# A state-space layer scanned token by token, and by chunks of four tokens

## The reference, cut to what matters

```python
lam_bar = jnp.exp(lam * dt)
b_bar = ((lam_bar - 1.0) / lam)[..., None] * b
bu = jnp.einsum('bsgh,gph->bsgp', uf, b_bar)
# states[t] = lam_bar * states[t-1] + bu[t], over 512 tokens
y = jnp.einsum('bsgp,ghp->bsgh', states, c).real + d_skip * uf
y = gelu(y)
```

## Time and profile before

| | |
|---|---|
| median of 3 runs | 3060.92 us (3058.44 to 3063.92) |
| the profiled execution | 3063.83 us |
| its span, first to last instruction | 3062.0 us |
| mean granted TensorE clock | 0.962 |
| TensorE busy | 2899.5 us (95%) |
| VectorE busy | 1527.1 us (50%) |
| ScalarE busy | 967.5 us (32%) |
| GpSimd busy | 175.9 us (6%) |
| state-space stage, 1966.57 to 2250.60 us | 284.03 us |
| in it: TensorE, VectorE, GpSimd busy | 238.09, 262.39, 131.75 us |
| in it: mean granted clock | 0.81 |

### The profile page before, as it was taken

One profiled execution on the slowest core, in us unless ns is written; L12 is line 12 of the kernel. 1 busy time (PEld: TensorE's weight loads), 2 busy tenths in 40 slices (PEclk: granted clock), 3 DMA queues, 4 the chain that ended last, 5 costly groups with the idle time before them and its releaser, 6 DMA issues.

```text
span 3062.0 us, 42173 instructions
## 1 busy us (share of the span) xinstructions
PE 2899.5 (95%) x17870; PEld 2326.6 (76%) x17870; DVE 1527.1 (50%) x2550; ACT 967.5 (32%) x1556; POOL 175.9 (6%) x136
## 2 busy tenths in 40 slices
PE   7999999999999999999999999788996899999999
PEld 5875678888888877767788888645574688888887
DVE  3464444433233344347565355599967633443333
ACT  2144543221122232146443233311125422332222
POOL 2000000100000000000000000154400000000000
PEclk9999999999999999999999999877877999999999
DMA  6232010222333211110112333011120032322322
GB/s 251 88 106 67 28 35 29 96 104 105 116 107 118 86 63 56 62 35 1 55 56 90 103 110 110 29 42 41 50 79 28 28 97 96 103 70 86 107 91 88
DMA packets 67787, 238.46 MB, mean 78 GB/s; under 512 B 7440, under 2 KB 10640, under 8 KB 66960
## 3 DMA queue, kind: packets, MB, share of 16 engines
q1 hardware_dynamic: 67312, 234.20, 22.5%
q10 hardware_dynamic: 288, 1.57, 0.2%
HBM read 233.64 MB, written 2.10 MB: 77 GB/s over the span
## 4 chain that ended last, share of the span: by engine, by line
PE 85%; DVE 10%; ACT 3%; issue 2%; DMA 1%; POOL 0%; SPq 0%; DVEq 0%; ACTq 0%; POOLq 0%
PE PSA L646 82%; PE PSA L952 1%; DVE WS L2071 1%; PE PSA L1213 1%; DVE Y L2693 1%; DMA Y<-in_early 1%; DVE Y L2690 1%; DVE stat L2774 1%; DVE Y L2689 1%; ACT Y L1939 0%; PE PSA L1447 0%; DVE HS L2241 0%; ACT WS L1532 0%; ACT Y L1946 0%; DVE Y L2703 0%
## 5 line engine op out<-in xcount | busy, mean ns | idle before, releaser
L646 PE MATMUL PSA<-HS,WS 128*128 128x512 f32 (+1 forms) x6672 | 1367.6, 366 | 19.2 <-DVE HS L2241 12.7
L646 PEld LDWEIGHTS PSA<-HS,WS 128*128 128x128 f32 x6672 | 1139.4, 191 | 250.8 <-issue 45.5
L2071 DVE TENSOR_TENSOR WS<-W,WS 128x1024 fp32r<-128x1024 f32 (+2 forms) x318 | 363.2, 1144 | 583.6 <-ACT WS L1532 582.4
L1532 ACT ACTIVATE WS<-W 128x1024 fp32r<-128x1024 f32 (+2 forms) x318 | 313.9, 989 | 846.9 <-PE PSA L646 487.6
L646 PE MATMUL PSA<-YS,WS 128*128 128x512 f32 (+1 forms) x2232 | 471.1, 372 | 3.5 <-DVE YS L2806 3.5
L646 PEld LDWEIGHTS PSA<-YS,WS 128*128 128x128 f32 x2232 | 393.1, 189 | 79.4 <-DVE YS L2806 3.9
L646 PE MATMUL PSA<-Y 128*64 128x128 f32 (+8 forms) x2048 | 319.7, 374 | 56.1 <-DVE Y L2703 36.5
L646 PEld LDWEIGHTS PSA<-Y 128*64 128x64 f32 (+3 forms) x2048 | 176.8, 164 | 153.1 <-issue 83.7
L1516 ACT ACTIVATE Y<-PSA 128x512 f32<-128x512 f32 (+3 forms) x73 | 50.2, 692 | 329.2 <-PE PSA L646 325.8
L646 PE MATMUL PSA<-HS,YS 128*128 128x512 f32 (+1 forms) x696 | 130.7, 346 | 4.5 <-issue 4.1
L646 PEld LDWEIGHTS PSA<-HS,YS 128*128 128x128 f32 x696 | 109.7, 194 | 22.7 <-issue 7.7
(11 more groups left out here) (298 smaller groups left out, 2586.6 us busy)
## 6 DMA issues: line engine op xcount, KB each, us to landing
W<-in_weights SPq DMA_DIRECT2D x396, 512.0 KB, 3.5
Y<-in_early SPq DMA_DIRECT2D x4, 2048.0 KB, 19.5
W<-in_weights SPq DMA_DIRECT2D x24, 256.0 KB, 2.7
X<-in_x SPq DMA_DIRECT2D x4, 768.0 KB, 20.4
W<-in_weights SPq DMA_DIRECT2D x24, 128.0 KB, 2.3
Y<-in_ssm ACTq DMA_DIRECT2D x1, 1024.0 KB, 7.2
out<-X SPq DMA_DIRECT2D x1, 1024.0 KB, 5.8
C<-in_consts SPq DMA_DIRECT2D x1, 948.5 KB, 33.0
```

The lines of the kernel that those rows point to most:

```text
L646: return pe.matmul(out, lhsT, rhs, start=first, stop=last)
L1532: act.activation(split_home(n)[:, 0, 0:f], W[:, c % W_RING, 0:f], ACT.Copy)\
L2071: tt(home[:, 1, 0:f], W[:, c % W_RING, 0:f], home[:, 0, 0:f].bitcast(F32), ALU.subtract)\
```

## The change

The 512 tokens are cut into 128 chunks of four. What four tokens bring into the state at a chunk's end is a sum over the four steps j, with the input matrix multiplied by the transition to the power 3 - j. TensorE makes that sum in PSUM (`chunk_inputs`), so that one state tile has 128 columns in place of 512, and the four state tiles of 128 channels are worked on together: `chunk_states(q)` on VectorE replaces four steps of before, with 8 scans of 128 columns. The output has two parts. From the state before the chunk comes the product with the output matrix times the transition to the power j + 1 (`OB`, made by GpSimd in `observe`). From the tokens inside the chunk comes a sum of lag matrices, one of 128 x 128 for each of the lags 0 to 3, which TensorE makes once (`lag_kernels`), ScalarE copies block by block (`keep_kernels`), and into whose lag 0 VectorE adds the skip as a diagonal (`add_skip`). `read_out(q)` adds both in one PSUM bank for four state tiles, and ScalarE takes it out with the gelu.

The input matrices of the four steps are made in feed-forward 1 on VectorE (`next_inputs`) and turned by TensorE there (`turn_inputs`, 32 transposes in place of 8), behind gate and up tiles 14, 15 and 17. The projection's tiles "q2" move behind "kc" and "vc". GpSimd makes 4 sets of phasors in place of 16, and 4 sets of output matrices. Tables move to other buffers.

```diff
-            state_inputs(0)
-            for i in range(SSM_T):
-                if i + 1 < SSM_T:
-                    state_inputs(i + 1)
-                for key in keys_at_state_tile(i):
-                    tile(key, ("in2",) + key, HS2, LAT)
-                read_out(i)
+            def chunk_inputs(q):
...
+                u = by_step(U[:, q, :])
                 for ri in range(2):
+                    for j in range(STEP):
+                        for r in range(4):
+                            key, rows = keys[r // 2], slice(32 * r, 32 * r + 32)
+                            at = S * (r % 2) + CHUNKS * ri
+                            ins = mm(PS[slot(key)][:, at:at + CHUNKS], BBT[rows, j, ri, q, :], u[rows, :, j],
+                                     j == 0, j == STEP - 1)
...
+            def lag_kernels():
...
+                for later in range(2):
+                    if later:
+                        pe.wait_ge(observed, value("observed", 2))
+                    for q in range(4):
+                        for ri in range(2):
+                            for r in range(4):
...
+                                if later:
+                                    ins = mm(half[:, 2 + q // 2::2, :], BB[:, ri, i, :], OB[:, 0:STEP - 1, ri, i, :],
+                                             ri == 0, ri == 1)
+                                else:
+                                    ins = mm(half[:, q // 2, :], BB[:, ri, i, :], SSMW[:, 2 + ri, i, :],
+                                             ri == 0, ri == 1)
...
+            def read_out(q):
...
+                ps, u = by_step(PS[slot(key)][:, 0:S]), by_step(U[:, q, :])
+                for l in range(STEP):
+                    mm(ps[:, :, l:STEP], lag_kernel(l, q), u[:, :, 0:STEP - l], l == 0, False)
+                pe.wait_ge(observed, value("observed", 3))
+                pe.wait_ge(states_ready, value("states_ready", q))
+                for j in range(STEP):
+                    for ri in range(2):
+                        for r in range(4):
+                            ins = mm(ps[32 * r:32 * r + 32, 1:CHUNKS, j], OB[:, j, ri, 4 * q + r, :],
+                                     XB[q % 2][:, ri, r * CHUNKS:(r + 1) * CHUNKS - 1],
+                                     False, j == STEP - 1 and ri == 1)
...
+            chunk_inputs(0)
+            for n, key in enumerate(IN2[4:28]):
+                tile(key, ("in2",) + key, HS2, LAT)
+                if n % 4 == 2 and n < 12:
+                    chunk_inputs(n // 4 + 1)
+                if n == 4:
+                    lag_kernels()
+                if n % 4 == 1 and 5 <= n <= 17:
+                    read_out(n // 4 - 1)
...
+                if n % 4 == 1 and 5 <= n <= 17:
+                    q = n // 4 - 1
+                    copy_out(("y", q), U[:, q, :], n=S, func=ACT.Gelu_apprx_tanh)
...
+            pool.wait_ge(b_bar, value("b_bar", 0))
+            pool.wait_ge(psum_filled[slot(last)], turn(last))
+            chunk_phasors(0)
+            pool.wait_ge(psum_filled[slot(("u", 3))], turn(("u", 3)))
+            chunk_phasors(1)
+            for j in range(STEP):
+                observe(j)
+            for q in (2, 3):
+                pool.wait_ge(states_ready, value("states_ready", q - 2))
+                chunk_phasors(q)
...
+            def chunk_states(q):
...
+                for h in range(2):
...
+                    tt(vr_, g[:, 0], er_, ALU.mult)
+                    tt(zi_, g[:, 0], ei_, ALU.mult)
+                    tt(zr_, g[:, 1], ei_, ALU.mult)
+                    tt(vi_, g[:, 1], er_, ALU.mult).then_inc(psum_drained[slot(key)], 1)
...
+                for t in range(4):
...
+                    dve.tensor_tensor_scan(zr[:, cols], decay, vr[:, cols], 0.0, ALU.mult, ALU.add)
+                    ins = dve.tensor_tensor_scan(zi[:, cols], decay, vi[:, cols], 0.0, ALU.mult, ALU.add)
...
+            for n, key in enumerate(IN2[4:28]):
+                if n % 4 == 0 and n < 16:
+                    chunk_states(n // 4)
+                in2(key)
+                if n == 4:
+                    add_skip()
```

More of the change, by code:

```diff
@@ L234, in build @@
         b_bar = sem("b_bar")
+        observed = sem("observed")
+        kernels_ready = sem("kernels_ready")
         branches_split = sem("branches_split")
@@ L1300, in _ @@
-            for ri in range(2):
-                pe.wait_ge(psum_drained[slot(("b_turned", ri))], turn(("b_turned", ri)))
-            def state_inputs(i):
-                q, rows = i // 4, slice(32 * (i % 4), 32 * (i % 4) + 32)
-                take(("bu", i))
-                if turn(("bu", i)) > 1:
-                    pe.wait_ge(psum_drained[slot(("bu", i))], turn(("bu", i)) - 1)
-                ps = PS[slot(("bu", i))]
-                for ri in range(2):
-                    ins = mm(ps[:, ri * S:(ri + 1) * S], BBT[rows, ri, q, :], U[rows, q, :], True, True)
-                ins.then_inc(psum_filled[slot(("bu", i))], 1)
@@ L1313, in read_out @@
-            def read_out(i):
-                pe.wait_ge(states_ready, value("states_ready", i))
-                rows = slice(32 * (i % 4), 32 * (i % 4) + 32)
-                take(("y", i))
-                if turn(("y", i)) > 1:
-                    pe.wait_ge(psum_drained[slot(("y", i))], turn(("y", i)) - 1)
-                ps = PS[slot(("y", i))]
-                for ri in range(2):
-                    ins = mm(ps[rows, 0:S], SSMW[:, 2 + ri, i, :], SB_[:, 8 + ri, :], ri == 0, ri == 1)
-                ins.then_inc(psum_filled[slot(("y", i))], 1)
@@ L1917, in _ @@
             more_weights(("cmp1", 1, 3))
-            for q in range(4):
-                act.wait_ge(psum_drained[slot(("y", 4 * q + 3))], turn(("y", 4 * q + 3)))
-                act.activation(U[:, q, :], U[:, q, :], ACT.Gelu_apprx_tanh).then_inc(ssm_out, one("ssm_out", q))
             act.wait_ge(psum_filled[slot(("kcmp",))], turn(("kcmp",)))
@@ L2698, in _ @@
+                link(ins)
+                read = ("cb", 0) if q < 2 else ("y", q - 2)
+                dve.wait_ge(psum_filled[slot(read)], turn(read))
                 tt(xr, zr, er, ALU.mult)
```

275 lines of the change are left out of this document (170 added, 105 removed).

## The result

The changed kernel takes 2974.44 us, median of 4 runs (2973.28 to 2976.32), against 3061.73 us for the kernel before on the same chip. The ratio is 0.9716, 95% interval 0.97 to 0.9733. The forecast was 2977 us. The profiled executions differ by as much: spans of 3062.0 and 2974.5 us.

What follows compares the result with a forecast made beforehand. VectorE was taken to bound the state-space stage before, TensorE after. New stage 181.3 + 10.1 + 5 = 196.4 us for 284.0, saving 87.6; feed-forward 1 adds 4.1; 2980.3 profiled, 2977 us as median, range 2955 to 3020.

Steps and rivals of the forecast that it cites:

- the sum by stretches: State-space stage 87.6 us shorter, 4.1 us added in feed-forward 1 for 32 transposes, nothing taken behind the stage.
- VectorE set the pace of the stage before: In the state-space stage before, VectorE was busy 262.39 of 284.03 us and TensorE waited 36.5 us for it.
- TensorE's work: In the new stage at full clock: projection tiles, chunk inputs, both read-out products and lag matrices, 181.3 us together.
- Both rivals on this block: On `chunk_inputs`: strided records take twice their time (16%, 3020 us); four row groups overlap, 7 us not 28 (9%, 2956).
- Strided operands: Rival, 16%: strided reads in chunk inputs and gapped PSUM writes in read-outs double such records' time, adding 43 us: 3020.
- Waits: TensorE's idle time left in the new stage, at its start, first read-out, ring slots and end: 10.1 us together.
- VectorE's set of 14.0 us: VectorE's work for four state tiles in the new stage: products, sums at 1.45 us, scans at 0.45 us, 14.0 us.
- The late-helper rival: Rival, 11%: GpSimd's sets take 15 us, TensorE waits 17 (2994); or 128-column scans cost as much as 512-column ones (3013).
- Clock: In the new stage, three of TensorE's waits may each cost 1.7 us of lowered clock: 5 us.
- the signs that the prediction named for being wrong: Idle TensorE ahead of `observed` or `weights_split`, half clock behind the small blocks, a VectorE set of over 16 us.
- Gain not there: Rival, 1%: VectorE remains the bound, which would need sets of some 60 us; about 3061 us.
- the half clock rival: Rival, 4%: small products put the stage at 1.2 GHz, 181 us of work become 362; the kernel ends at 3153.

Runs made afterwards that it cites:

- group_by_group: The changed kernel with the chunk sums' loops turned round, all four steps of one 32-row group before the next: 2998.27 us, ratio 0.9795 to the kernel before.

## Why the prediction was right, point by point

- **The time** of 2977 was 2.6 us off, and the sum by stretches came out close as well: stage -90.3 against -87.6, the start of the stage +4.9 against +4.1, behind it -2.1 against 0. That the last two agree says little, as they are within what one execution differs from the next. What was forecast right is the mechanism, VectorE's work off the path and TensorE the bound; that the number came within 3 us is luck, as the points below show.
- **VectorE set the pace of the stage before**: shown. Without its scans the kernel is 41 us faster, without most of GpSimd's work beside it 43, and the first of these edits takes only 5 from the changed kernel.
- **TensorE's work**, 181.3 us, was 15 too much. The tiles, 129.6, measured 5.47 us each, 131.3. The lag products, 9.1, measured 10.0; the state products, 9.6, measured 7.5; the lag matrices, 4.8, measured 2.0. The term that was mis-sized is `chunk_inputs`: 28.2 us (110 ns a record), measured 15.3 (60 ns). The nearest row had two row groups in turn, and I took its price for four. Both rivals on this block were true at once: four groups run together (31 ns a record with whole runs, 8.0 us in all, where that rival had 7), and the strided operand doubles it. Each multiplied the wrong base, so that neither gave the time.
- **Strided operands** cost 4 x 1.82 us on the chunk inputs and 4 x 0.25 on the lag products, 8 us, not 43. The Trainium skill's rule on lines of 16 bytes in SBUF ("SBUF — State Buffer", section "Door 1: The DMA port swizzle") agrees with 60 against 31 ns. Its sentence there that any gap in PSUM slows matmuls significantly does not agree with the trace: 1.94 us with and without.
- **Waits**, 10.1 us, measured 21.6: 11.2 for the skip (3.5 predicted), 5.9 for a split (none, "covered, narrowly"), 2.8 for ring slots (3.4), 1.8 at the end (2.3), none at the start (0.9; the first products want only u0, long copied). The step that failed is VectorE's set of 14.0 us. Its sums at 1.45 had GpSimd's delay in them and its scans at 0.45 had not. Alone it takes 10.6 us (the third set, from 2060.89 to 2071.5), beside GpSimd 24. The late-helper rival named GpSimd's own set (8.4 us taken; 7.5 to 10.8 in the trace) and long scans; it did not name what happened, that GpSimd at work makes each operation beside it wait.
- **Clock**, 5 us: two tiles lost 2.4 and the lag products 1.8 behind the long waits, 4.2. Work, waits and clock so measured come to 191.9 of the 193.7 us.
- So the two mis-sized terms cancelled: 15 us less work, 11.5 us more waits. The forecast was good to 3 us with terms wrong by four to five times that. Of the signs that the prediction named for being wrong, two came true, TensorE idle ahead of `weights_split` (5.9 us) and a set on VectorE of over 16 us (24), and VectorE was busy for 114.6 us where 92 were worked out. They cost TensorE waits at the start of the stage and did not make VectorE the bound again.
- **Gain not there, and half clock**: neither. The granted clock in the stage rose to 0.95. The drop that the half clock rival feared behind small products did come in group_by_group, with the row groups one after the other.

## What to carry to other kernels

Ask of each duration that you take from a trace what ran on GpSimd beside it: an operation of VectorE that reads two tensors from SBUF, here also one with a tensor and a scalar, costs one price alone and another, higher by a nearly fixed sum, in company, and many short ones pay that sum many times. Move such a helper to where less waits for VectorE before shaving the waited-for engine's own work: here 8 us less work on TensorE shortened the stage by 4.6 us with the helper in the way and by 8.0 with it gone. Matmuls of 32 rows are cheapest when the four row groups are issued in turn and the moving operand is a whole run.

## What the runs showed of the hardware

- Beside a working GpSimd, VectorE's operations with two SBUF operands last mostly 0.7 to 1.1 us longer, and no more for a long one than for a short one: a scan of 128 columns 1.20 for 0.39 us, of 512 columns 1.96 for 1.23, a product of 512 columns 1.53 for 0.69. A `TENSOR_SCALAR` of 512 columns lasted 1.49 for 0.48. A product with one operand from PSUM stays at 0.41. GpSimd's own operations stretch too, from 1.05 to 2.1 us. The Trainium skill says it in "SBUF — State Buffer", section "Who interferes with whom": a VectorE instruction with two SBUF inputs contends with a GpSimd instruction that reads SBUF, by a lock held for the whole instruction and not by a share of the bandwidth. The trace agrees: the sum does not grow with the length, and the product from PSUM stays at 0.41. I had not drawn on it.
- 64 products of 32 rows and 128 columns: 2.0 us with four row groups in turn and whole runs, 3.8 with a stride of 16 bytes, 9.2 with that stride and one group after the other, the last in part at half clock.
- Left open: the skip's operations were about 1.24 us each in every run that was looked at, with the last phasor set begun just ahead of them. Starting it behind them was not tried. Nor was it looked for why the stretches outside the stage differ by 2 to 6 us between executions.
